# One block for sparse attention and the RWKV recurrence: the recurrence's elementwise first stage placed among the sample value products

## The reference

```python
def ab_mixer(h, e, dsa_fn, shift_prev, S0, P):
    z = h @ P['ab_w_in'][e]
    q, k, v, qi, ki, wi, zb = split_cols(z, [...])
    ya = dsa_fn(e, q, k, v, qi, ki, wi)...      # scores of an index, top-k keys, softmax, p @ v over the paged cache
    yb, shift_new, S_new = rwkv7(zb, shift_prev, S0, e, P)
    y = jnp.concatenate([ya, yb], axis=-1) @ P['ab_w_out'][e]

def rwkv7(zb, shift_prev, S0, e, P):
    prev = jnp.concatenate([shift_prev[:, None], zb[:, :-1]], axis=1)
    z = zb + (prev - zb) * P['rwkv_mu'][e]                                   # token shift
    r, k, v, xw, xa, xg = split_cols(z, ...)
    w_log = -softplus(-(w0 + tanh(xw) @ w2)) - 0.5;  decay = exp(-exp(w_log))
    a = sigmoid(a0 + xa @ a2);  g = sigmoid(xg) @ g2
    kk = k * kkw;  kk = kk * rsqrt(max(sum(kk * kk), 1e-24))                 # per head
    k = k * (1 + (a - 1) * ka)
    # scan over time: S = S * w + (S @ -kk) (kk * a)^T + v k^T;  y = S @ r
    y = head_norm(y, lnx_g, lnx_b) + sum(r * k * rk) * v
    return y * g, zb[:, -1], S_fin
```

## Time and profile before

| | busy us | share of the span |
|---|---|---|
| PE | 1456.4 | 90% |
| PEld | 1310.9 | 81% |
| DVE | 1120.5 | 69% |
| ACT | 310.0 | 19% |
| POOL | 314.0 | 19% |

### The profile page before, as it was taken

The page is one execution under the profiler, slowest core; times in us unless marked ns, Lnnn a source line. Parts: engine busy times, 40 slices in busy tenths (PEclk is TensorE's granted clock), DMA queues, the critical chain, the costliest instruction groups (busy, mean ns, idle before and its releaser), DMA issues. The chain is left out here.

```text
span 1616.5 us, 27957 instructions
## 1 busy us (share of the span) xinstructions
PE 1456.4 (90%) x11270; PEld 1310.9 (81%) x11270; DVE 1120.5 (69%) x1439; ACT 310.0 (19%) x597; POOL 314.0 (19%) x289
## 2 busy tenths in 40 slices
PE   6999999998986688499999989999999696899997
PEld 6999999974331477389999989999896465899996
DVE  6877767638852643769776688768572967797764
ACT  3111120004321412132211131110201321311200
POOL 2433110001000000034331143321200101343310
PEclk9999999998988698799999999999999778999998
DMA  7442715628763000345435534426161204544242
GB/s 289 150 162 78 258 62 182 216 97 287 268 223 130 1 3 6 130 176 183 163 122 188 192 116 164 174 87 241 34 229 39 84 30 182 201 158 156 78 161 84
DMA packets 63721, 233.74 MB, mean 145 GB/s; under 512 B 9675, under 2 KB 19568, under 8 KB 46476
## 3 DMA queue, kind: packets, MB, share of 16 engines
q1 hardware_dynamic: 51722, 225.82, 39.1%
q10 hardware_dynamic: 11554, 6.37, 1.3%
q0 software_dynamic: 352, 0.23, 0.0%
HBM read 226.06 MB, written 6.10 MB: 144 GB/s over the span
## 5 line engine op out<-in xcount | busy, mean ns | idle before, releaser
L185 PE MATMUL psum<-x_hi_r,pair_hi 128*128 128x288 f32 x1744 | 519.6, 298 | 37.7 <-DVE ring_r L180 37.7
L187 PE MATMUL psum<-x_hi_r,ring_r 128*128 128x288 f32 x1744 | 518.6, 297 | 0.0
L186 PE MATMUL psum<-x_lo_r,pair_hi 128*128 128x288 f32 x1616 | 477.8, 296 | 0.0
L185 PEld LDWEIGHTS psum<-x_hi_r,pair_hi 128*128 128x128 f32 x1744 | 331.4, 190 | 40.5 <-DVE ring_r L180 40.0
L187 PEld LDWEIGHTS psum<-x_hi_r,ring_r 128*128 128x128 f32 x1744 | 330.9, 190 | 0.0
L180 DVE TENSOR_TENSOR ring_r<-ring,pair_hi 128x2048 fp32r<-128x2048 f32 x127 | 327.7, 2581 | 4.3
L186 PEld LDWEIGHTS psum<-x_lo_r,pair_hi 128*128 128x128 f32 x1616 | 305.6, 189 | 0.4
L185 PE MATMUL psum<-hidden_hi_r,down_hi 128*128 128x288 f32 x704 | 208.4, 296 | 0.0
L186 PE MATMUL psum<-hidden_r,down_hi 128*128 128x288 f32 x704 | 207.7, 295 | 0.0
L187 PE MATMUL psum<-hidden_hi_r,down_r 128*128 128x288 f32 x704 | 207.0, 294 | 0.0
L171 DVE CAST pair_hi<-ring 128x2048 fp32r<-128x2048 f32 x127 | 159.7, 1257 | 34.6 <-DMA ring<-in_w_gu 16.8
(11 more groups left out here) (516 smaller groups left out, 1814.4 us busy)
## 6 DMA issues: line engine op xcount, KB each, us to landing
ring<-in_w_gu SPq DMA_DIRECT2D x88, 1024.0 KB, 4.8
down<-in_w_down SPq DMA_DIRECT2D x64, 704.0 KB, 4.2
ring<-in_w_ab SPq DMA_DIRECT2D x18, 1024.0 KB, 5.0
ring<-in_w_cd SPq DMA_DIRECT2D x13, 1024.0 KB, 6.3
ring<-in_cache_k SPq DMA_DIRECT2D x32, 256.0 KB, 4.9
index_keys<-in_cache_k SPq DMA_DIRECT2D x32, 256.0 KB, 4.4
index_keys<-in_cache_i ACTq DMA_DIRECT2D x64, 64.0 KB, 2.7
eight_pages_ds<-in_cache_v SPq DMA_DIRECT2D x16, 256.0 KB, 5.9
```

Source lines behind the costliest of these rows:

```text
L185: pe.matmul(out, w_hi, x_hi, start=start, stop=False)
L186: pe.matmul(out, w_hi, x_lo, start=False, stop=False)
L187: return pe.matmul(out, w_lo, x_hi, start=False, stop=stop)
```

## The change

The recurrence has no block of its own any more. `rwkv_stage` becomes `recurrence(...)`, which returns functions, one for each part of each engine's list; `dsa_stage` calls them in its one block. Arithmetic and instruction shapes are as before. The order of the engines' lists becomes:

- PE: `weights_transposed(0)`; b0 = 0, with `weights_transposed(1)` after its fourth page; `decay_products` (L1087's four, L1096's four); b0 = 2, with `rate_products` (L1089's) after the fourth page; b0 = 4, with `key_norms` (L1100's) after the fourth page; b0 = 6; `value_products` (L1092's and the transposes of v); both `heads_transposed`; `chunk_products` (the rest, from the transposes of BK).
- ACT: copies of the first weights; tanh and sigmoid; copies of the second weights; square, sigmoids, square root, exponentials; the copies of the two sums; the gate's copies and the rest.
- DVE: after `divided(1)` the whole elementwise first stage, then the copies into `ymix`, then the rest.
- POOL: eight constant loads (`first_loads`) as soon as the index weights are done, ahead of its eight plus three DMAs for the top-k of the samples; the load of `wa2` and the zeroing of AR, BK and U at its end.
- SP: `pair_rows` before the last four half loads of value pages; g2 and the state s0t after the pages of b0 = 4 and b0 = 6 are used; then the stores.

Buffers that had their own room lie in dead ones: D and the low-rank inputs in z[0:16], f1 to f3 in one tile with qi, qz, iss and rank, PW, PWT, U and g2 in the index keys, s0t, AKV and ST in `eight_pages`, others in the attention's masks.

```diff
             for b0 in range(0, NB, 2):
                 g = b0 // 4
                 for b in (b0, b0 + 1):
                     pe.wait_ge(kv_landed[VALUE_SLOTS[b]], 128 * VALUE_LOADS[b])
-                if b0 % 4 == 0:
-                    weights_transposed(g)
-                    pe.wait_ge(S["st_out"], 3 * g + 3)
+                if b0 == 0:
+                    weights_transposed(0)
+                pe.wait_ge(S["st_out"], 3 * g + 3)
...
-                    if b0 == 0 and j == 3:
-                        mm.then_inc(S["kv_used"], 1)
+                    if j == 3:
+                        if b0 == 0:
+                            mm.then_inc(S["kv_used"], 1)
+                            weights_transposed(1)
+                        if b0 == 2:
+                            rk.rate_products(pe)
+                        if b0 == 4:
+                            rk.key_norms(pe)
...
-                if b0 == 4:
-                    heads_transposed(0)
+                if b0 == 0:
+                    rk.decay_products(pe)
+            rk.value_products(pe)
+            heads_transposed(0)
             heads_transposed(1)
+            rk.chunk_products(pe)
...
+            weights_out(0)
+            rk.lora_inputs(act)
+            weights_out(1)
+            rk.lora_out(act)
+            rk.decays(act)
+            values_out(0)
+            values_out(1)
+            rk.chunks_out(act)
...
             divided(1)
+            rk.inputs(dve, ln)
             for g in range(2):
                 dve.wait_ge(S["pv_sum"], g + 1)
...
+            rk.chunks(dve, ln)
...
             pool.memset(qz[:, :, :, :], 0.0).then_inc(S["qz_zero"], 1)
+            rk.first_loads(pool)
...
+            rk.lora_loads(pool)
+            rk.zeros(pool)
...
             load_halves("cache_v", 4, VALUE_SLOTS, 8)
+            rk.rows_load(sp)
             load_halves("cache_v", 6, VALUE_SLOTS, 10)
+            sp.wait_ge(c.stored, 48)
             sp.wait_ge(S["ki_done"], 1)
             c.store(sp, c.outs["kidx"], ki[0:64])
+            rk.last_loads(sp)
+            rk.stores(sp)
             stores_done(c, sp)
...
+    def first_loads(pool):
+        pool.wait_ge(A["wi_done"], 1)
+        for dst, src in ((par..., "rk_par"), (shiftT, "shiftT"), (seg, "seg"), (pair_cols, "pair_cols"), (bmask, "bmask"),
+                         (id2, "id2"), (amask, "amask"), (gmask, "gmask")):
+            pool.dma_start(dst, c.ins[src]).then_inc(S["mix_loaded"], 16)
+    def zeros(pool):
+        pool.wait_ge(A["kv_used"], NB + 3)
+        pool.memset(AR[:, :, :, NT:NP_], 0.0)...; pool.memset(BK[:, :, 4, :, NS:L], 0.0)...
+        pool.wait_ge(A["kv_used"], NB + 4)
+        pool.memset(U[:, :, :, :, :], 0.0)...
+    def last_loads(sp):
+        sp.wait_ge(A["kv_used"], NB + 4)
+        sp.dma_start(g2, c.ins["g2"])...
+        sp.wait_ge(A["kv_used"], NB + 5)
+        sp.dma_start(s0t, c.ins["s0t"])...
+    def decay_products(pe):
+        pe.wait_ge(S["mix_loaded"], 16 * 9); pe.wait_ge(A["st_out"], 6); pe.wait_ge(S["lora_in"], 2)
+        ...                               # 4 products of w2; wait for the square; 4 column sums
+    def rate_products(pe):                # 4 products of a2, each after the sigmoid that frees its bank
+    def key_norms(pe):
+        pe.wait_ge(S["lora_out"], 2 * HP); pe.wait_ge(S["par_loaded"], 16); pe.wait_ge(S["kk_rows"], 1)
+        ...                               # 4 row products
+    def value_products(pe):
+        pe.wait_ge(S["par_loaded"], 32); pe.wait_ge(S["ar_done"], 1)
+        ...                               # 4 products of g2; wait for lora_out 12; the transposes of v
```

More of the change, by code:

```diff
@@ L1 @@
+from collections import namedtuple
 from contextlib import ExitStack
@@ L767, with recurrence @@
 EXP_HALF = float(np.exp(-0.5))
-def rwkv_stage(c, z, vtok, ymix):
+Recurrence = namedtuple("Recurrence", (
+    "first_loads", "lora_loads", "zeros", "rows_load", "last_loads", "stores", "inputs", "chunks", "lora_inputs", "lora_out", "decays", "chunks_out",
+    "decay_products", "rate_products", "key_norms", "value_products", "chunk_products"))
+def recurrence(c, z, ymix, idx, A, par, zlast, shared, pages):
     nc = c.nc
-    c.limit = nc.sbuf_top
     S = {}
@@ new lines, in rate_products @@
+    def rate_products(pe):
+        for h in range(HP):
+            pe.wait_ge(S["lora_out"], h + 1)
+            pe.matmul(free[h][:, 0:NT], wa2[64:128, h * P:h * P + P], z[64:128, Z_WA], start=True, stop=True).then_inc(S["lora_sum"], 1)
+    def key_norms(pe):
+        pe.wait_ge(S["lora_out"], 2 * HP)
+        pe.wait_ge(S["par_loaded"], 16)
+        pe.wait_ge(S["kk_rows"], 1)
+        for h in range(HP):
+            pe.matmul(free[h][:, 0:NT], pair_rows[:, h], rows8, start=True, stop=True).then_inc(S["kk_all"], 1)
@@ new lines, in value_products @@
+    def value_products(pe):
+        pe.wait_ge(S["par_loaded"], 32)
+        pe.wait_ge(S["ar_done"], 1)
+        for h in range(HP):
+            pe.matmul(free[h][:, 0:NT], g2[:, h * P:h * P + P], lw[:, 1], start=True, stop=True).then_inc(S["lora_sum"], 1)
+        pe.wait_ge(S["lora_out"], 3 * HP)
+        pe.wait_ge(S["mixed"], 14)
+        for c_ in range(CH):
+            n = L if c_ < 4 else NS
+            if c_ >= 3:
+                pe.wait_ge(S["act_out"], c_ - 2)
+            for q in range(2):
+                lo = (1 - q) * 64
+                for h in range(HP):
+                    mm = pe.matmul(B[1 + c_ % 3][lo:lo + n, h * L:h * L + L], v[:, h, c_ * L:c_ * L + n],
+                                   c.ident[:, half(q)], start=True, stop=True)
+            mm.then_inc(S["act_grp"], 1)
@@ new lines, in chunk_products @@
+        pe.wait_ge(S["ss_out"], HP)
+        for h in range(HP):
+            pe.wait_ge(S["yc_sq"], h + 1)
+            mm = pe.matmul(B[4][0:8, 0:NT], pair_cols[:, h], f2[:, h], start=(h == 0), stop=(h == HP - 1))
+        mm.then_inc(S["var_sum"], 1)
+        pe.wait_ge(S["var_rows"], 1)
+        for h in range(HP):
+            pe.matmul(B[4 + h][:, 0:NT], pair_rows[:, h], rows8, start=True, stop=True).then_inc(S["var_all"], 1)
+    return Recurrence(first_loads=first_loads, lora_loads=lora_loads, zeros=zeros, rows_load=rows_load, last_loads=last_loads, stores=stores,
+                      inputs=inputs, chunks=chunks, lora_inputs=lora_inputs, lora_out=lora_out, decays=decays, chunks_out=chunks_out,
+                      decay_products=decay_products, rate_products=rate_products, key_norms=key_norms, value_products=value_products,
+                      chunk_products=chunk_products)
@@ L1347, in dsa_stage @@
         eight_pages = sb("eight_pages", [P, NPG, 512])
+        rk = recurrence(c, z, ymix, idx, S, par, zlast, shared, eight_pages)
         KEY_SLOTS = (0, 1, 2, 3, 0, 1, 2, 3)
```

862 lines of the change are left out of this document (414 added, 448 removed).

## The result

The kernel with the change took 1580.53 us (median of 4 runs, 1578.03 to 1583.95), the kernel before 1617.87 us beside it: a ratio of 0.9767, interval 0.975 to 0.9784. The predicted 1584.0 has a ratio of 0.979, just outside; the mechanism of the likeliest case was right, and the forecast gain of 34.3 us was 3.0 short of the 37.3 measured here, and 4.0 to 4.5 short of the 38.3 and 38.8 of two later series. The profiled execution took 1578.03 us, the least of the four, and its span is 1576.2 us.

What follows compares the result with a forecast made beforehand. Value products (PE) and the recurrence's first stage (mostly DVE, ACT) lay one behind the other. Overlapped, the first chunk product moves from 564.22 to 529.9, 34.3 us less: 1618.3 - 34.3 = 1584.0 us, range 1580.5 to 1591.

Steps and rivals of the forecast that it cites:

- likeliest case: First stage runs beside PE's value products: 34.3 us less, 1584.0 us, own range 1581.5 to 1589.5, chance 0.80.
- walk of PE's list: PE's new order checked at each wait, from first value product at 473.9 to first chunk product at 529.9 us.
- transposes of v: PE, in value_products after b0 = 6: 4.3 us at full clock, where 5.95 was seen partly at 0.50 clock.
- transposes of BK: Twenty on PE just ahead of the first chunk product: five times 0.66 is 3.3, taken as 3.4 us.
- column sums: PE, behind decay_products and ahead of b0 = 2, waiting for ACT's square: 2.1 us.
- stall of 0.6 for the square: PE waits 0.6 us after the decay products, from 487.2 to 487.8, until ACT's square is handed over.
- The forecast told in parts: 44.3 us chain leaves the path, 8.5 us of products go among the value products, 2.59 us load wait goes.
- Room at the meeting points: PE reaches the norm products 3.6 us after the reciprocal is ready, and value_products 4.9 us after AR.
- Rival A: PE stands at a meeting point for a late input: 3 to 5 us at one, say 1590, chance 0.10.
- Rival B: The recurrence's remainder or the projection also runs faster with the upper clock: 1 to 4 us more, 1579, chance 0.05.
- Rival C: POOL's eight loads hold up the top-k DMAs: slower than before, 1632 at 10 us a load, chance 0.03.
- Rival D: A new wait is met only when the value products end, so no overlap: 1616 to 1618, chance 0.02.

Runs made afterwards that it cites:

- filler12: The changed kernel with twelve more DVE operations (9.63 us in all, results unused) ahead of the reciprocal for the norm products: 1589.9 us, ratio 0.9839.
- filler_busy: The changed kernel with twelve added DVE operations ahead of the reciprocal and 18 unread PE products ahead of the norm products: 1586.93 us, ratio 0.9789.
- serial: The changed kernel with only the overlap undone, the first stage's calls standing behind the value products again: 1616.24 us, ratio 0.9981.
- akv_warm_short: The changed kernel with the five AKV copies on ACT, plus unread PE products in the tail's gaps and 30 heading the projection: 1579.63 us, ratio 0.9755.
- after_third: The changed kernel unaltered, run once more in the same rounds as later candidates: 1580.97 us against 1619.22, ratio 0.9768.
- warm_short: The changed kernel with unread PE products in the tail's gaps, 16 behind the last norm and 30 heading the projection: 1578.8 us, ratio 0.9753.
- double: The changed kernel with the transposes of v and BK issued twice and the column sums repeated in b0 = 2 and b0 = 4: 1594.38 us, ratio 0.9845.
- akv_act: The changed kernel with the five AKV copies moved from DVE to ACT: 1582.24 us, ratio 0.977.

## Why the mechanism was right and the time wrong

- *What bounds the kernel, and the mechanism:* right. Undoing the overlap alone gives 34.8 of the 38 us back. The failed step is in the walk of PE's list: the prices of its own small terms.
- *The walk, as offsets from the first value product, forecast and measured:* end of b0 = 0 11.3 and 11.9 (the clock rose later); rates 19.5 and 18.6; end of b0 = 2 26.1 and 25.2; of b0 = 4 36.3 and 35.4; of b0 = 6 44.2 and 43.4; transposes of v 47.1 and 46.1, their end 51.4 and 49.7; back-transposes' end 52.6 and 50.7; first chunk product 56.0 and 53.0. These are the first profile's; in the other two b0 = 0 ended at 11.4 and 11.0 and the first chunk product came at 52.5.
- *The terms that were too dear,* which are the step that failed: **transposes of BK**, 3.4 against 2.36 from start to start (1.0); **transposes of v**, 4.3 against 3.60 (0.7); the **column sums** behind decay_products, 2.1 ahead of b0 = 2 against 0.98 (the first pages begin 0.98 us behind them and run beside them) (1.1); the stall of 0.6 for the square, which was 0.0 to 0.3 in the change's profiles (but up to 0.74 in kernels with the same list up to there, see the last section); back-transposes, 1.2 against 0.93 (0.3). With the 0.6 lost in b0 = 0 and 0.1 in small ones they make the 3.0 us that the walk was long (3.5 in the other two profiles).
- *Why BK was too dear:* I took five times a duration of 0.66 for four transposes. A group's duration holds one tail, and that was multiplied too. Two sizes of the same operation in the earlier trace rows part them: nine in 1.20 and four in 0.66 make (1.20 - 0.66) / 5 = 0.108 each and 0.23 of tail, so twenty take 2.4, and 2.43 was measured. The 4.3 for v was not the plain scale of its row, as the text has it (2560 of 1152 columns times 2.21 is 4.9), and the text doesn't say what was taken off.
- *The forecast told in parts* doesn't add up by itself: 44.3 + 2.6 - 8.5 is 38.4, not 34.3. It leaves out what else lay in that chain and stays in PE's list (the gate products with their wait and the transposes of v, 7.2 in the walk, and the stall), and some 3.5 us the other way (the rest of the time between the blocks, two short waits, the cheaper transposes of BK). The walk itself adds up.
- *Room at the meeting points:* right to 0.2 us, 3.8 and 5.1 measured against 3.6 and 4.9, with some luck: both sides of each point came 0.8 to 1.0 us earlier than forecast. **Rival A** did not occur in the change; its price of 3 to 5 us for one point is shown too low: 4.2 us of waiting cost 8.3 to 8.8.
- *The clock:* as forecast, 1.00 in every window from 480 to 540 in the change's three profiles; three kernels with the same list up to that point show 0.72 to 0.87 in 485 to 490. The Trainium skill (TensorE: Matmul & The Clock Gate, Part 1: The HAM clock gate) says that activity releases the upper level. filler12 agrees: the clock was 0.50 in 505 to 515 behind a wait of 4.22 us and 1.00 again in 520 to 525. filler_busy shows a fall that this sentence doesn't explain, to 0.66 in 510 to 515, behind a stretch in which PE was busy 4.82 of 5 us.
- *Bounds and range:* the lower end, 1580.5, allowed for stall, handoffs and an earlier clock in the remainder, but gave none of the PE terms a lower bound. So the measured time fell on the end of the range and below the likeliest case's own 1581.5. With the five terms as measured the sum would have been 1580.3, and 1581.0 with the 0.7 us that went the other way.
- ***Rival B*:** not what happened. The remainder gave 0.3 to 0.8 us, but for one profile with 2.8. **Rival C:** 0.54 us a load, and the top-k's DMAs start within 0.3 us of where they did. **Rival D:** serial shows what it would have been, 1616.24; all new waits were met inside the value products.

## What to carry to other kernels

Where two engines take turns in long pieces, walk the in-order list of the one that is to stay busy and compare, at every meeting point, when each side is there; here that placed six points within a microsecond. Take a product's price from two group sizes in the trace (the slope), and give each price a lower bound as well as an upper one: prices that are all rounded up add to a bias. A stall on PE can cost twice its length or more (4.2 us cost 8.3 to 8.8), so the rooms of 3.8 and 5.1 us are worth keeping when the kernel is changed again, and the square for the column sums, which has almost none (see the next section), is the first place to make some.

## What the runs showed that I had not expected

- Small products ran beside large ones that write other columns of the array: the column sums (8 columns from column 0) ahead of b0 = 2, whose products go to columns 64 to 127, held them up by 0.98 us, and the two groups overlap in the timeline; beside b0 = 4, which writes 0 to 63, they cost 1.93 and nothing overlaps. The two places differ in more than the columns (ahead of the first page, behind the second), and the columns weren't changed alone.
- The square has almost no room, and what there is goes when PE's clock rises early. Eleven profiles have the same lists up to the column sums. The start of the decay products, counted from the first value product, moved from 10.5 to 12.1 us with the clock in b0 = 0. Where it came at 11.3 or later PE didn't wait for the square; at 11.2 it waited about 0.1 us (akv_warm_short), between 11.0 and 10.8 it waited 0.29 (after_third), 0.31 (warm_short), 0.38 (double) and 0.41 us (akv_act), at 10.5 it waited 0.74 (filler_busy). Behind the waits up to 0.31 the granted clock stayed 1.00 in 485 to 490; behind the other three it was 0.87, 0.82 and 0.72, and in akv_act the stretch to AKV came out 1.1 to 1.6 us longer. That the short wait brought the clock down was not tried by itself.
- The tail of the recurrence ran at either clock level in executions of one and the same kernel: the four mean products took 4.21 us in the change's first profile and 2.21 in the second and third, and the way from AKV to the square root that opens the next block 97.6 and then 94.5 and 94.1 us. That is 3 us of scatter that no edit made, as large as what the last experiments were after.
